# A transformer kernel: smaller first transfers, one scaled half of the values behind a copy, and one group of transposes inside a sum

## The chip, the cores and the metric

The kernel runs on one core of one Trainium2 chip. A core has five engines that run in parallel and meet only at semaphores: TensorE (PE in the profile; its weight loads are PEld), VectorE (DVE), ScalarE (ACT), GpSimd (POOL) and SyncE (SP, which here only issues DMAs). The metric is the device time of one execution in microseconds (us), as the median of several runs.

## The reference, cut to what matters

One call computes a 256 x 1024 activation in fp32 through a feed-forward layer, a mixer of chunked attention and pooling, a second feed-forward layer, and then two more mixers with layer norms: "Fox" attention and "DSA" attention.

```python
x = x + 0.5 * swiglu_ffn(rmsnorm(x, ffn1_norm), w_gate, w_up, w_down)     # starts the kernel
x = x + hybrid_mixer(rmsnorm(x, mix_norm), ...)
x = x + 0.5 * swiglu_ffn(rmsnorm(x, ffn2_norm), ...)
x = rmsnorm(x, final_norm)
# Fox: 8 heads of 128
q, k, v, f_logit, gate = split(x @ fox_w_in)
s = q @ k.T * scale + cum_q - cum_k            # causal
o = softmax(s) @ v
x = layer_norm(DN_ALPHA * x + (silu(gate) * o) @ fox_w_out)
# DSA: top-k selected attention
x = layer_norm(DN_ALPHA * x + dsa_mixer(x))
```

The three places of the change are the very first products (x @ w_gate and x @ w_up), the values v of Fox, and the sum with `fox_w_out` with the transposes of the normalised rows that follow it.

## The kernel before, in words

**Products.** Every fp32 product is made of three: an operand is split into a high part (ACT copies it to a reduced fp32 type: `hi`, `whi`) and the rest (DVE or POOL subtracts: `lo`, `wlo`). A helper `three` makes high x high, high x rest, rest x high. Weights come in chunks of 1 MB, 128 partitions x 2048 columns, into a ring of four buffers `raw`; SP issues a chunk when the rest of the chunk four before it has been made (`lo_ready`), ACT makes `hi` when the chunk has landed and PE has used the chunk four before, DVE makes `lo` behind it, and PE takes the chunk. All engines execute their own program in order: an instruction that waits holds up everything behind it on its engine.

**The start.** The first two chunks (c = 0 and 1) are worked together in pieces along k, the 8 blocks of 128 rows of the contraction: `PIECES = [(0, 1), (1, 1), (2, 2), (4, 2), (6, 2)]`, each a first k and a count. `STEPS` goes over the pieces, and in each over the two chunks. The input arrives already turned, `x_turned`, in four transfers of two k each (256 KB). ACT scales k into `xth` (L1108), DVE makes `xtl` (L1527), ACT makes the piece's `whi` for c = 0 and then for c = 1 (L1213), DVE the two `wlo` (L1651), and PE multiplies in `first_pair` (L585 high, L601 rest). The first weight piece, both chunks together (256 KB), is issued on ACT's queue behind the small constants `sm`; everything else on SP's. While it waits PE executes 9 products of zeros (L660). After the first pair come chunk 2 in two halves, chunk 3, and then the loop. Inside chunk 3 PE turns the row norms into a row (`rstd_to_row`, L505), ACT copies it out of bank 7 (`row`, L1113), and PE waits for that copy (`row_ready`, L572) before it sums into the same bank. On ACT the copy stands behind `hi` of the fifth chunk (L1080).

**Fox attention.** For head h PE makes the scores (`scores2`, L825), DVE adds the bias, negates and takes the row's extreme (`causal`, L1629), ACT makes the exponentials (`exps`, L1183), PE turns them (`turn_probs`, L654), DVE copies them to SBUF (`probs_out`, L1637), and PE multiplies with v (`values2`, L709 to L711). The order on PE is scores of h + 1, turn of h, values of h - 1. v is scaled by the row norms when it leaves PSUM: the first 128 tokens by ACT, the other 128 by DVE (`values_out`, L1798), each in two halves of 512 columns: heads 0 to 3 and heads 4 to 7.

**The end of Fox.** `end_sums` (L517) adds the last half of the contraction for the output matrix in four groups (token tile t, column half nb) of 4 k. Behind it follow the layer norm on DVE (L1884, L1888), transposes of the normalised rows on PE (`turn_y`, L880, four per half), `xth` by ACT (L1343) and `xtl` by DVE (L1844), and then the first DSA product (`one_tile`), which waits for the first half of the parts before k = 0 and for the second before k = 4.

Of the kernel before, what the change touches and what calls it, by code (L numbers as in the profile page):

```python
# [28 lines left out]
KD = D // P  # L29
# [84 lines left out]
def build(nc, a, out):  # L114
    ctx = ExitStack()
    with ctx:
# [133 lines left out]
        sm_landed, xt_landed = sem("sm_landed"), [sem(f"xt_landed{i}") for i in range(KD // 2)]  # L250
# [55 lines left out]
        def _(sp):  # L306
# [15 lines left out]
            def x_piece(k):  # L322
                sp.dma_start(x_turned[:, k:k + 2, :], a["xt"][:, k:k + 2, :]).then_inc(xt_landed[k // 2], 16)
# [6 lines left out]
            weight_piece(1)  # L330
            for i in range(2, len(PIECES) - 1):
                x_piece(PIECES[i][0])
                weight_piece(i)
            x_piece(PIECES[-1][0])
# [67 lines left out]
        def _(pe):  # L402
# [114 lines left out]
            def end_sums(c0, between=None):  # L517

                for t in range(NT):
                    for nb in range(2):  # L520
                        wh, wl = take(c0 + nb)
                        for k in range(HALF):
                            if between and t == 1 and nb == 1 and k == 2:
                                between()
                            m = three(ps[:, 2 * nb + t, :],
                                      xth[:, HALF + k, t * P:(t + 1) * P], xtl[:, HALF + k, t * P:(t + 1) * P],
                                      wh[:, k * BANK:(k + 1) * BANK], wl[:, k * BANK:(k + 1) * BANK], False, k == HALF - 1)
                        m.then_inc(chunk_used if t else acc_part, 1)
# [130 lines left out]
            for _ in range(9):  # L659
                pe.matmul(ps[:, DOWN + 3, 0:P], idle, idle, start=True, stop=True)  # L660
# [187 lines left out]
            def values2(h):  # L848
                if h == 0:
                    pe.wait_ge(v_act, 2)  # L850
                    pe.wait_ge(v_dve, 2)
# [31 lines left out]
            end_sums(C_FO + 2, lambda: turn_y(0, 0))  # L883
            turn_y(0, 1)
# [186 lines left out]
        def _(act):  # L1071
# [145 lines left out]
            cols = first_cols(0)  # L1217
# [4 lines left out]
            for step, (c, i) in enumerate(STEPS):  # L1222
                k, n = PIECES[i]
                if c == 0:
                    act.wait_ge(xt_landed[k // 2], 16)
                    input_hi(0, k, n)
                part_high(c, slice(k * S, (k + n) * S), step if step < N_PARTS else None,
                          part_landed[i] if step < N_PARTS else raw_landed[c], raw_first[:, first_cols(i, c)])
# [278 lines left out]
        def _(dve):  # L1507
# [149 lines left out]
            for step, (c, i) in enumerate(STEPS):  # L1657
                k, n = PIECES[i]
                if c == 0:
                    dve.wait_ge(xt_landed[k // 2], 16)  # L1660
# [151 lines left out]
            values_out(1)  # L1812
# [12 lines left out]
            for h in range(H2):  # L1825
                if h >= 2:
                    causal(h)
                if h >= 1:
                    probs_out(1, h - 1, 2 + (h - 1) % 2)
                if h == 7:  # L1830
# [375 lines left out]
```

## Time and profile before

| | us |
|---|---|
| median of 3 runs | 711.37 |
| lowest and highest of the 3 | 709.96, 712.58 |
| the profiled execution's own time | 709.67 |
| its span on the core | 707.9 |

| engine | busy us | share of the span |
|---|---|---|
| PE | 697.5 | 99% |
| DVE | 480.0 | 68% |
| ACT | 378.3 | 53% |
| POOL | 54.4 | 8% |

The busy time of PE counts overlapping products, so 99% does not say that no stall is left; stalls are found where the start of one product stands further from the start of the one before than its columns explain, or in the idle time that the profile prints in brackets. The granted clock of TensorE is full in all 40 slices of the page. The rows of the places that the change touches stand in a section of their own below.

### The profile page before, as it was taken

The numbers are of one execution on the slowest core, as the hardware profiler recorded it, in microseconds if no ns is written. First come the engines' busy times: TensorE is split into PE (matmuls) and PEld (weight loads), VectorE is DVE, ScalarE is ACT, GpSimd is POOL, SyncE is SP. The second block draws the span as 40 slices with busy tenths as digits, with TensorE's granted clock in tenths as the row PEclk, the third lists the DMA queues.
The fourth block names the chain that finished last, engine by engine and source line by source line (L and its number), as shares of the span: only waits on it lengthen the run. The fifth ranks groups of instructions, "written<-read, shape, count | busy, mean of one in ns | idle before, by whom it ended". The sixth has DMA issues, their size and how long they took to land.

```text
span 707.9 us, 9725 instructions
## 1 busy us (share of the span) xinstructions
PE 697.5 (99%) x3728; PEld 594.3 (84%) x3728; DVE 480.0 (68%) x724; ACT 378.3 (53%) x517; POOL 54.4 (8%) x32
## 2 busy tenths in 40 slices
PE   8999999999999999999999999999999999999995
PEld 7888888888888788888888888888888888888884
DVE  6797777755476556777667755566763738888756
ACT  6865445444377655744455544477444534675450
POOL 0000000000000400000000000000005172130001
PEclk9999999999999999999999999999999999999999
DMA  8987555555355324655455555535573183444001
GB/s 326 357 339 280 203 182 178 186 201 207 119 187 229 120 78 139 258 209 179 178 186 197 205 208 219 177 134 223 186 259 145 42 315 123 176 145 153 1 1 59
DMA packets 21107, 129.33 MB, mean 183 GB/s; under 512 B 2504, under 2 KB 3664, under 8 KB 6864
## 3 DMA queue, kind: packets, MB, share of 16 engines
q1 hardware_dynamic: 19728, 127.51, 49.9%
q10 hardware_dynamic: 1344, 1.34, 0.6%
q8 instruction: 23, 0.38, 0.2%
q14 instruction: 12, 0.10, 0.0%
HBM read 127.79 MB, written 1.06 MB: 182 GB/s over the span
## 4 chain that ended last, share of the span: by engine, by line
PE 98%; DVE 1%; DMA 1%; ACT 0%; issue 0%; ACTq 0%
PE ps L440 24%; PE ps L405 16%; PE ps L407 16%; PE ps L406 16%; PE ps L446 13%; PE ps L425 1%; PE ps L654 1%; PE ps L585 1%; PE ps L1006 1%; PE ps L825 1%; PE ps L459 1%; PE ps L429 1%; DMA raw<-in_first 1%; PE ps L709 1%; PE ps L601 1%; PE ps L710 1%
## 5 line engine op out<-in xcount | busy, mean ns | idle before, releaser
L1514 DVE TENSOR_TENSOR wlo<-raw,whi 128x2048 fp32r<-128x2048 f32 x69 | 159.1, 2313 | 40.7 <-ACT whi L1080 40.5
L440 PE MATMUL ps<-xt,whi 128*128 128x512 f32 x752 | 180.1, 391 | 0.0
L1080 ACT ACTIVATE whi<-raw 128x2048 fp32r<-128x2048 f32 x78 | 148.6, 1908 | 44.9 <-PE ps L407 42.1
L440 PEld LDWEIGHTS ps<-xt,whi 128*128 128x128 f32 x752 | 138.1, 188 | 26.7
L405 PE MATMUL ps<-whi,xt 128*128 128x512 f32 (+1 forms) x304 | 121.6, 400 | 0.1
L407 PE MATMUL ps<-whi,xt 128*128 128x512 f32 (+1 forms) x304 | 116.9, 385 | 0.0
L406 PE MATMUL ps<-wlo,xt 128*128 128x512 f32 (+1 forms) x304 | 116.7, 384 | 0.0
L446 PEld LDWEIGHTS ps<-xt,wlo 128*128 128x128 f32 x752 | 96.4, 191 | 3.7
L446 PE MATMUL ps<-xt,wlo 128*128 128x256 f32 x752 | 97.5, 283 | 0.0
L1467 POOL TENSOR_TENSOR wlo<-raw,whi 128x2048 fp32r<-128x2048 f32 (+1 forms) x9 | 41.1, 4561 | 550.6 <-ACT whi L1080 550.6
L1124 ACT ACTIVATE work<-ps 128x512 f32<-128x512 f32 x44 | 26.2, 597 | 95.1 <-PE ps L440 94.8
L405 PE MATMUL ps<-whi,hth 128*128 128x512 f32 x192 | 75.2, 391 | 0.0
L406 PE MATMUL ps<-wlo,hth 128*128 128x512 f32 x192 | 74.7, 389 | 0.0
L407 PE MATMUL ps<-whi,htl 128*128 128x512 f32 x192 | 74.7, 389 | 0.0
L1597 DVE TENSOR_TENSOR wlo<-raw,whi 128x2048 fp32r<-128x2048 f32 x32 | 73.3, 2292 | 1.5
L405 PEld LDWEIGHTS ps<-whi,xt 128*128 128x128 f32 x304 | 57.2, 188 | 12.4 <-issue 1.7
L407 PEld LDWEIGHTS ps<-whi,xt 128*128 128x128 f32 x304 | 57.1, 188 | 11.7
L406 PEld LDWEIGHTS ps<-wlo,xt 128*128 128x128 f32 x304 | 57.3, 188 | 10.3 <-issue 0.2
L1555 DVE TENSOR_TENSOR work<-ps,work 128x512 f32<-128x512 f32 x44 | 30.2, 689 | 45.5 <-ACT work L1124 45.4
L1159 ACT ACTIVATE whi<-raw 128x2048 fp32r<-128x2048 f32 x32 | 61.1, 1909 | 0.0
L407 PEld LDWEIGHTS ps<-whi,htl 128*128 128x128 f32 x192 | 36.0, 188 | 7.5
L405 PEld LDWEIGHTS ps<-whi,hth 128*128 128x128 f32 x192 | 36.1, 188 | 7.4
(235 smaller groups left out, 692.9 us busy)
## 6 DMA issues: line engine op xcount, KB each, us to landing
raw<-in_gu SPq DMA_DIRECT2D x41, 1024.0 KB, 4.8
raw<-in_dn SPq DMA_DIRECT2D x22, 1024.0 KB, 4.8
raw<-in_win SPq DMA_DIRECT2D x8, 1024.0 KB, 4.8
raw<-in_fqk SPq DMA_DIRECT2D x8, 1024.0 KB, 4.8
raw<-in_wout SPq DMA_DIRECT2D x4, 1024.0 KB, 5.0
raw<-in_fg SPq DMA_DIRECT2D x4, 1024.0 KB, 4.8
raw<-in_fv SPq DMA_DIRECT2D x4, 1024.0 KB, 4.8
raw<-in_fo SPq DMA_DIRECT2D x4, 1024.0 KB, 4.9
```

The lines of the kernel that those rows point to most:

```text
L405: pe.matmul(o, xh, wh, start=start, stop=False)
L406: pe.matmul(o, xh, wl, start=False, stop=False)
L407: return pe.matmul(o, xl, wh, start=False, stop=stop)
L440: return pe.matmul(ps[:, banks[u], :], wh[:, k * S + u * P:k * S + (u + 1) * P], x, start=k == 0, stop=k == KD - 1)
L446: pe.matmul(ps[:, banks[u], S:2 * S], wl[:, k * S + u * P:k * S + (u + 1) * P], xth[:, k, :], start=False, stop=False)
L1080: act.activation(whi[:, c % RING, 0:n], raw[:, c % RING, 0:n], ACT.Copy).then_inc(hi_ready, 1)
L1124: act.activation(gu_sb[:, i % 2, :, :], ps[:, 2 * i:2 * i + 2, S:2 * S], ACT.Copy).then_inc(cross_copied, 1)
L1159: act.activation(whi[:, c % RING, :], raw[:, c % RING, :], ACT.Copy).then_inc(hi_ready, 1)
L1467: pool.tensor_tensor(wlo[:, c % RING, 0:n], raw[:, c % RING, 0:n], whi[:, c % RING, 0:n].bitcast(F32), ALU.subtract).then_inc(lo_ready, 1)
L1514: dve.tensor_tensor(wlo[:, c % RING, 0:n], raw[:, c % RING, 0:n], whi[:, c % RING, 0:n].bitcast(F32), ALU.subtract).then_inc(lo_ready, 1)
L1555: dve.tensor_tensor(g, ps[:, 2 * i:2 * i + 2, 0:S], g, ALU.add).then_inc(gu_read, 1)
L1597: dve.tensor_tensor(wlo[:, c % RING, :], raw[:, c % RING, :], whi[:, c % RING, :].bitcast(F32), ALU.subtract).then_inc(lo_ready, 1)
```

## The change

1. **First step.** The input's transfers follow `PIECES`, so k = 0 and k = 1 come as 128 KB each instead of 256 KB together. The first weight piece is split by chunk: c = 0 (128 KB) stays on ACT's queue, c = 1 (128 KB) goes to SP's with a semaphore of its own, `second_landed`. PE executes 10 products of zeros instead of 9.
2. **Fox values.** DVE's scaling of the second half of v (`values_out(1)`) moves from before the first copy of turned probabilities to behind it, and PE's wait for the second half moves from head 0 to head 4, the first that reads it.
3. **Transposes.** In the last group of `end_sums` the second half's transposes `turn_y(0, 1)` come before k = 3 instead of behind the group; those of the first half stay before k = 2.

```diff
-        sm_landed, xt_landed = sem("sm_landed"), [sem(f"xt_landed{i}") for i in range(KD // 2)]
+        sm_landed, xt_landed = sem("sm_landed"), [sem(f"xt_landed{i}") for i in range(len(PIECES))]
+        second_landed = sem("second_landed")
...
-            def x_piece(k):
-                sp.dma_start(x_turned[:, k:k + 2, :], a["xt"][:, k:k + 2, :]).then_inc(xt_landed[k // 2], 16)
+            def x_piece(i):
+                k, n = PIECES[i]
+                sp.dma_start(x_turned[:, k:k + n, :], a["xt"][:, k:k + n, :]).then_inc(xt_landed[i], 16)
...
             x_piece(0)
-            weight_piece(1)
-            for i in range(2, len(PIECES) - 1):
-                x_piece(PIECES[i][0])
+            cols = first_cols(0, 1)
+            sp.dma_start(raw_first[:, cols], a["first"][:, cols]).then_inc(second_landed, 16)
+            for i in range(1, len(PIECES) - 1):
+                x_piece(i)
                 weight_piece(i)
-            x_piece(PIECES[-1][0])
+            x_piece(len(PIECES) - 1)
...
-                            if between and t == 1 and nb == 1 and k == 2:
-                                between()
+                            if between and t == 1 and nb == 1 and k >= 2:
+                                between(k - 2)
...
-            for _ in range(9):
+            for _ in range(10):
...
-                if h == 0:
+                if h == H2 // 2:
                     pe.wait_ge(v_act, 2)
                     pe.wait_ge(v_dve, 2)
...
-            end_sums(C_FO + 2, lambda: turn_y(0, 0))
-            turn_y(0, 1)
+            end_sums(C_FO + 2, lambda half: turn_y(0, half))
...
-            cols = first_cols(0)
+            cols = first_cols(0, 0)
             act.dma_start(raw_first[:, cols], a["first"][:, cols]).then_inc(part_landed[0], 16)
...
             causal(0)
             causal(1)
-            values_out(1)
...
                     probs_out(1, h - 1, 2 + (h - 1) % 2)
+                if h == 1:
+                    values_out(1)
```

The transfers that SP issues first, before the change (128x512 is 256 KB; `work<-in_xt` is the input, `raw<-in_first` the weight pieces):

```order
1 L323 DMA work<-in_xt 128x512
2 L327 DMA raw<-in_first 128x512
3 L323 DMA work<-in_xt 128x512
4 L327 DMA raw<-in_first 128x1024
5 L323 DMA work<-in_xt 128x512
6 L327 DMA raw<-in_first 128x1024
```

and after it:

```order
1 L325 DMA work<-in_xt 128x256
2 L333 DMA raw<-in_first 128x256
3 L325 DMA work<-in_xt 128x256
4 L329 DMA raw<-in_first 128x512
5 L325 DMA work<-in_xt 128x512
6 L329 DMA raw<-in_first 128x1024
```

SP issues two transfers more ahead of the two-k pieces, and four transfers of the start are now 128 KB: these three and ACT's.

DVE at the end of `causal(1)`, before the change (the ISA rows are `causal`, COPY is `probs_out(0)`, TENSOR_SCALAR is `values_out(1)`):

```order
293 L1629 ISA work,st<-ps,gains 128x256
294 L1629 ISA st 128x1
295 L1798 TENSOR_SCALAR work<-ps,st 128x512
296 L1637 COPY work<-ps 128x384
297 L1629 ISA work,st<-ps,gains 128x128
```

and after it:

```order
293 L1631 ISA work,st<-ps,gains 128x256
294 L1631 ISA st 128x1
295 L1639 COPY work<-ps 128x384
296 L1800 TENSOR_SCALAR work<-ps,st 128x512
297 L1631 ISA work,st<-ps,gains 128x128
```

The copy and the scaling have changed places; both still stand ahead of `causal(2)`.

PE in the last group of `end_sums`, before the change (X is turned by the rows of 128x128 x4; 128x232 is the first DSA product):

```order
1332 L880 MATMUL ps<-eye,X 128x128 x4
1333 L405 MATMUL ps<-whi,xt 128x512
1334 L406 MATMUL ps<-wlo,xt 128x512
1335 L407 MATMUL ps<-whi,xt 128x512
1336 L405 MATMUL ps<-whi,xt 128x512
1337 L406 MATMUL ps<-wlo,xt 128x512
1338 L407 MATMUL ps<-whi,xt 128x512
1339 L880 MATMUL ps<-eye,X 128x128 x4
1340 L405 MATMUL ps<-whi,xt 128x232
```

and after it:

```order
1332 L883 MATMUL ps<-eye,X 128x128 x4
1333 L408 MATMUL ps<-whi,xt 128x512
1334 L409 MATMUL ps<-wlo,xt 128x512
1335 L410 MATMUL ps<-whi,xt 128x512
1336 L883 MATMUL ps<-eye,X 128x128 x4
1337 L408 MATMUL ps<-whi,xt 128x512
1338 L409 MATMUL ps<-wlo,xt 128x512
1339 L410 MATMUL ps<-whi,xt 128x512
1340 L408 MATMUL ps<-whi,xt 128x232
```

The second four transposes stand three products earlier.

## Rows read from the trace of the kernel before

**Rows 1.** The page: busy time per engine, and the chain that ended last.

```profile
PE 697.5 (99%) x3728; PEld 594.3 (84%) x3728; DVE 480.0 (68%) x724; ACT 378.3 (53%) x517; POOL 54.4 (8%) x32
...
PE 98%; DVE 1%; DMA 1%; ACT 0%; issue 0%; ACTq 0%
```

**Rows 2.** Timeline of the start: start us, duration us, engine, line, tiles, [idle before <-releaser].

```profile
5.08 0.51 ACT L1108 ACTIVATE xt<-work,sm 128x256 fp32r<-128x256 f32 x1 [1.91 <-DMA sm<-in_sm]
...
6.21 0.72 ACT L1213 ACTIVATE whi<-raw 128x256 fp32r<-128x256 f32 x2 [0.62 <-DMA raw<-in_first]
...
6.77 0.70 PE L585 MATMUL ps<-xt,whi 128*128 128x512 f32 x2 [1.76 <-ACT whi L1213]
...
9.66 1.08 PE L585 MATMUL ps<-xt,whi 128*128 128x512 f32 x4
```

**Rows 3.** The same timeline: transfers that SP issues.

```profile
2.13 0.43 SPq L327 DMA_DIRECT2D raw<-in_first  x1
...
6.93 0.94 SPq L343 DMA_DIRECT2D X<-in_x  x2
7.91 0.45 SPq L344 DMA_DIRECT2D eye<-in_eye  x1
...
14.55 0.96 SPq L319 DMA_DIRECT2D raw<-in_gu  x2
```

**Rows 4.** DMAs by stretch of issue: count, KB each, us to landing; last, instruction fetches 20.3 to 21.5.

```profile
raw<-in_first SPq DMA_DIRECT2D x1, 512.0 KB, 6.3
...
X<-in_x SPq DMA_DIRECT2D x1, 512.0 KB, 13.2
...
eye<-in_eye SPq DMA_DIRECT2D x1, 128.0 KB, 13.1
...
raw<-in_gu SPq DMA_DIRECT2D x1, 1024.0 KB, 9.7
...
q8 instruction: 1, 0.02, 5.6%
```

**Rows 5.** Timeline of chunk 3: ACT's copy of the row, PE's load behind it.

```profile
24.27 1.91 ACT L1080 ACTIVATE whi<-raw 128x2048 fp32r<-128x2048 f32 x1 [0.93 <-DMA raw<-in_gu]
...
25.44 1.64 PE L425 MATMUL ps<-xt,whi 128*128 128x512 f32 x6
26.09 0.37 ACT L1113 ACTIVATE work<-ps 128x256 f32<-128x256 f32 x1
...
26.51 0.19 PEld L425 LDWEIGHTS ps<-xt,whi 128*128 128x128 f32 x1
```

**Rows 6.** Timeline of Fox heads 0 to 2.

```profile
551.72 0.49 PE L654 MATMUL ps<-eye,work 128*128 128x128 f32 x3
551.92 0.75 DVE L1798 TENSOR_SCALAR work<-ps,st 128x512 f32<-128x512 f32 x1 [4.85 <-PE ps L407]
552.59 0.55 DVE L1637 COPY work<-ps 128x384 f32<-128x384 f32 x1
553.05 0.28 DVE L1629 CUSTOM_DVE_ANT_0 work<-ps,gains 128x128 f32<-128x128 f32 x1
553.25 0.30 PEld L709 LDWEIGHTS ps<-work 128*128 128x128 f32 x2 [0.29 <-issue]
...
554.17 0.19 ACT L1183 ACTIVATION_READ_ACCUMULATOR work<-work,st 128x1 f32 x1
...
554.68 0.49 PE L654 MATMUL ps<-eye,work 128*128 128x128 f32 x3
```

**Rows 7.** Timeline of the end of Fox and the first DSA product.

```profile
586.63 0.75 DVE L1888 SCALAR_TENSOR_TENSOR X<-X,st,gains 128x512 f32<-128x512 f32 x1
...
588.35 0.60 PE L880 MATMUL ps<-eye,X 128*128 128x128 f32 x4
...
589.62 0.69 DVE L1844 TENSOR_TENSOR xt<-ps,xt 128x512 fp32r<-128x512 f32 x1 [0.48 <-ACT xt L1343]
...
590.36 0.19 PEld L405 LDWEIGHTS ps<-whi,xt 128*128 128x128 f32 x1 [0.27 <-DVE xt L1844]
```

More of the change, by code:

```diff
@@ L1224, in _ @@
                 if c == 0:
-                    act.wait_ge(xt_landed[k // 2], 16)
+                    act.wait_ge(xt_landed[i], 16)
                     input_hi(0, k, n)
                 part_high(c, slice(k * S, (k + n) * S), step if step < N_PARTS else None,
-                          part_landed[i] if step < N_PARTS else raw_landed[c], raw_first[:, first_cols(i, c)])
+                          second_landed if step == 1 else part_landed[i] if step < N_PARTS else raw_landed[c], raw_first[:, first_cols(i, c)])
             part_high(2, slice(0, D), N_PARTS, part_landed[len(PIECES) - 1], raw[:, 2, 0:D])
@@ L1659, in _ @@
                 if c == 0:
-                    dve.wait_ge(xt_landed[k // 2], 16)
+                    dve.wait_ge(xt_landed[i], 16)
                     input_lo(0, k, n)
```

## The prediction, made before the changed kernel was run

> **What bounds the kernel now.** I read four views in this order. The page comes first, for who holds the end: the chain that ended last is PE for 98% of the span, and PE's busy time is 99% of it [rows 1]. So only what moves PE's stream counts, and there is little idle time left to win. Then the timeline at the three places of the change, to find PE's stalls there: 1.76 us before the first product [rows 2], 0.29 us before the first product with v [rows 6], and 0.27 us in the first DSA product [rows 7]. Then the DMA view, for when transfers land. Last, the timeline from each place onwards, for the next wait that PE meets: a gain that arrives at a wait which is not itself moved is taken back there. That last look changes the result at the start.
>
> **First step, its own gain.** ACT scales k = 0 at 5.08, released by `sm`, a 24 KB transfer that the change leaves where it is; the first weights land at 6.2 (ACT resumes at 6.21 after 0.62 of idle), and PE starts at 6.77 [rows 2]. With 128 KB of weights on each queue instead of 256, I place their landing at about 5.4 to 5.6: half the bytes, at the rate that I work out below, are 0.33 us less for each of the two pieces that share the engines, and the input's half piece ahead of them another 0.33 at most. The input's path (5.08 plus the 1.69 from there to PE, less the 0.6 us for which ACT sat idle between) then allows PE at about 6.2. The fall is 0.5 to 0.6 us.
>
> PE is not free to run from there. The two-k weight piece was issued at 2.13 and landed 6.3 later, at 8.4 [rows 3, 4]; the same bytes stand ahead of it after the change. PE began on it at 9.66 [rows 2]. Its high part for c = 0 needs about 0.65 us of ACT after 8.4, so PE can begin no earlier than about 9.2: **at most 0.46 us** is left at this point.
>
> **First step, what takes it back.** In chunk 3 PE waits for ACT's copy of the norm row, since it sums into the same bank. That copy stands on ACT behind `hi` of the fifth chunk, which ran from 24.27, when the chunk had landed (0.93 of idle before it, released by the DMA), for 1.91 us; the copy ran from 26.09 to 26.46, and PE's next weight load starts at 26.51 [rows 5]. The group of six products ends at 27.08 and one lasts 0.39, so the sixth starts at 26.69, no later than its pitch asks: the wait costs nothing now but sits exactly at PE's heels. After the change PE arrives 0.46 earlier, ACT does not: the fifth chunk is issued at 14.55 and lands 9.7 later, at 24.25 [rows 3, 4], at the end of a queue that has been full since the start. When PE has waited, the product goes almost with its load, so the sixth can go at 26.54: about **0.14 us** of the 0.46 survives.
>
> The landing itself moves too, the wrong way. Four 128 KB transfers with 1 KB rows replace two 256 KB ones with 2 KB rows. The nearest row is `eye`, 128 KB in 1 KB rows: issued at 7.91, landed at 21.0, where the second half of X, issued at 7.42, landed at 20.6 [rows 3, 4]. That is 0.4 us, with 0.1 of rounding. Between the landings at 8.4 and 20.6 lie 4.5 MB, 2.7 us for 1 MB or 0.33 us for 128 KB. So a 1 KB-row piece costs 0 to 0.17 us more, four of them 0 to 0.7 us at the bounds; I take 0.15 in all, from the lower part, since the first two land while the engines aren't yet filled. First step together: -0.14 + 0.15, **about 0**.
>
> The Trainium skill's page "DMA: Bandwidth & Descriptors", section "Why small descriptors are slow (HBM only)", speaks against this part of the change: each packet carries about 3 cycles beside one per 32 bytes. By that, an estimate: 35 cycles instead of 32 for 1 KB, 67 instead of 64 for 2 KB, 4.5% of the 1.3 us of those 512 KB, 0.06 us; the sum below would then be 0.09 lower. No row of before shows it finer than the 0.1 of `eye`.
>
> The tenth product of zeros ends about 0.2 us later than the ninth; PE idles 1.76 us there [rows 2], so it is hidden, and would not be if data came before 5.3.
>
> **Fox values.** Now: DVE is released at 551.92, scales the second half of v until 552.67, copies the turned probabilities of head 0 from 552.59 to 553.14, starts `causal(2)` at 553.05, and PE loads for the values of head 0 at 553.25 after 0.29 idle [rows 6]. After: the copy waits for PE's transposes, which end at 552.21 [rows 6], runs 552.25 to 552.80, and PE, free to load at 552.96 (553.25 less the idle 0.29), doesn't wait: about 0.25 us gained. But `causal(2)` still stands behind both operations, and these no longer start at 551.92 but at 552.25. It starts at 552.25 + 0.47 + 0.67 = 553.39, 0.34 later than now. Behind it hang ACT's exponentials of head 2, done 1.31 us after `causal(2)` began (553.05 to 554.36), and PE's transposes of head 2, now 0.32 after that, at 554.68, with no wait [rows 6]. A load follows by 0.11 what it waited for (553.25 behind the copy's end at 553.14), and the product by some hundredths, so the transposes go at 553.39 + 1.31 + 0.15 = 554.85. The stall of 0.25 is gone, one of 0.48 stands a head later, net +0.17. In the heads behind, DVE has more to do per head than PE (copy, `causal`, a reciprocal and two gates) and sets the pace, and part of its own delay is made up while it waits for PE's scores before `causal(3)`. Carrying the starts of both engines through heads 3 to 6 leaves, by my estimate, half of the 0.17: **+0.09 us**. Bounds: -0.25, if the delay of `causal(2)` is hidden, and +0.17.
>
> **Transposes.** Now the second four transposes stand at 588.35, DVE makes the rest at 589.62 after 0.48 idle, and PE's load for k = 4 starts at 590.36 after 0.27 idle, released by it [rows 7]. Three products of 0.23 earlier, they go at about 587.65. The normalised half is ready at 586.63 + 0.75 = 587.38 [rows 7], and PE's load comes at 587.43: they pass with 0.05 to spare. The rest then is ready near 589.8, and PE reaches k = 4 at 590.12. The first half isn't touched, and PE's own work is the same, so the stall goes and nothing takes its place: **-0.24 us**, bounds -0.27 and 0. Nothing waits behind the group's end in these 0.44 us: the residual of its columns is later on DVE.
>
> **The sum.** 0 + 0.09 - 0.24 = -0.15 us. The profiled execution took 709.67, its span 707.9; it would become 709.5. The median of the three runs is 711.37, 1.7 above the profiled execution, and I apply the difference to it: **711.2 us**. The three runs lie 2.6 us apart, far more than the effect.
>
> **Rivals.**
>
> *The fifth chunk lands in time.* An instruction fetch of 16 KB kept one DMA engine busy at 20.4 for about 1 us (5.6% of 16 engines over 1.2 us) [rows 4], which is a reason why that landing is late. If the fetch falls elsewhere, the copy of the row comes earlier and the full 0.46 survives: -0.46 + 0.09 - 0.24 = -0.6, 710.8 us. Against it: the fetch follows the program, and that is nearly the same. Chance 0.2.
>
> *Slower: 1 KB rows cost as much as 2 KB rows.* Then 512 KB of the start take the time of 1 MB, 1.3 us more, the fifth chunk lands 1.3 later, and PE stalls for it at the row copy: -0.14 + 1.3 + 0.09 - 0.24 = +1.0, 712.4 us. It turns the result from a delay of the landing of 0.3 us. `eye` speaks against the full price, not against a third of it. Chance 0.15.
>
> *Fox gains.* ACT's exponentials hide the later `causal(2)`: 0 - 0.25 - 0.24 = -0.5, 710.9 us. Against it: the exponentials follow within 0.3 us of it. Chance 0.1.
>
> *The transposes don't do what they are moved for.* The second normalised half comes more than 0.05 late and PE waits in the middle of the group, which ends the sum later and delays the first half too: the 0.24 is not gained, +0.1, 711.5 us. Chance 0.1.
>
> *The forecast.* 711.2 us, chance 0.45.
>
> **The numbers.** All cases lie between 710.8 and 712.4. The scatter of a median is added: the three runs stand 1.4 below and 1.2 above theirs. I give 709.4 to 712.9. A measurement of this kernel can tell about 0.5%, 3.6 us, from no change; no case reaches it, so faster 0.03, same 0.95, slower 0.02 for what I haven't seen.
>
> **What the next profile would show.** Right: first product near 6.2; the two-k piece begun near 9.2; the weight load behind ACT's copy of the row now with idle time of some 0.3 before it, and PE's place there within 0.2 us of today's; no idle before the values of head 0, but one of 0.4 to 0.5 before the transposes of head 2; no idle before k = 4 of the first DSA product. Wrong: the loop's first product more than 0.3 us earlier or later than today, the transposes of head 2 without a wait, or a wait of PE inside the last group of `end_sums`. A difference of medians above 2 us would say that something else moved.

## The result, and the profile after

| | before | after |
|---|---|---|
| median, us (10 runs each, same chip) | 711.28 | 712.62 |
| lowest and highest | 709.62, 712.58 | 710.46, 713.04 |
| profiled execution | 709.67 | 713.01 |
| its span | 707.9 | 711.2 |

The ratio after to before is 1.0025, 95% interval 1.0015 to 1.0034. The change made the kernel 1.3 us slower. The time lies inside the range, but the forecast was 0.15 us faster, and the measurement excludes that: it tells 0.1% apart, where the prediction had allowed for 0.5%.

**The page.** PE still holds the end, as in [rows 1]. In the chain that ended last, by line, the first weights have a share of 1%, as they have before: a loss of this size doesn't show on the page, and the places of the change have to be read one by one.

```profile
PE 699.3 (98%) x3730; PEld 596.0 (84%) x3730; DVE 480.2 (68%) x724; ACT 378.7 (53%) x517; POOL 54.4 (8%) x32
...
PE ps L443 24%; PE ps L408 16%; PE ps L410 16%; PE ps L409 16%; PE ps L449 13%; PE ps L428 1%; PE ps L657 1%; DMA raw<-in_first 1%; PE ps L588 1%; PE ps L1008 1%; PE ps L462 1%; PE ps L432 1%; PE ps L828 1%; PE ps L517 0%; PE ps L712 0%; PE ps L713 0%
```

**The start.** The timeline of the changed kernel, answering to [rows 2] (columns as there; L588 is the high product, L1110 ACT's scaling of the input, L1215 its high part of the weights):

```profile
3.41 0.51 ACT L1110 ACTIVATE xt<-work,sm 128x256 fp32r<-128x256 f32 x1 [0.23 <-DMA sm<-in_sm]
...
4.34 0.72 ACT L1215 ACTIVATE whi<-raw 128x256 fp32r<-128x256 f32 x2 [0.43 <-DMA raw<-in_first]
4.50 2.15 SPq L325 DMA_DIRECT2D work<-in_xt  x1
...
5.34 0.71 PE L588 MATMUL ps<-xt,whi 128*128 128x512 f32 x2
...
9.49 0.91 ACT L1110 ACTIVATE xt<-work,sm 128x256 fp32r<-128x256 f32 x2 [3.39 <-DMA work<-in_xt]
...
10.80 1.15 ACT L1215 ACTIVATE whi<-raw 128x512 fp32r<-128x512 f32 x2 [0.40 <-DMA raw<-in_first]
...
11.58 1.55 PE L588 MATMUL ps<-xt,whi 128*128 128x512 f32 x4 [3.20 <-ACT whi L1215]
```

The first product goes 1.43 us earlier than before (5.34, 6.77). The piece behind it goes 1.92 later (11.58, 9.66): PE has used up k = 0 and k = 1 and sits idle for 3.20 us, because both the input and the weights for k = 2, 3 are late. ACT waits 3.39 us for the input, scales it, and waits 0.40 more for the weights, until 10.80; that wait ends last. The input is the transfer that SP issued at 1.66 before, and issues at 2.60 now. The DMA view, for transfers issued at those two moments (KB, us from issue to landing), before and then after, and last the weights, issued at 3.08 after:

```profile
work<-in_xt SPq DMA_DIRECT2D x1, 256.0 KB, 5.3
```

```profile
work<-in_xt SPq DMA_DIRECT2D x1, 256.0 KB, 6.9
```

```profile
raw<-in_first SPq DMA_DIRECT2D x1, 512.0 KB, 7.7
```

The input landed at 7.0 before and lands at 9.5 now; the weights landed at 8.4 [rows 3, 4] and land at 10.8. The busy time by stretch (us, then PE, PEld, DVE, ACT, POOL, the granted clock, the DMA engines' share, GB/s) tells more, before and then after:

```profile
4.50:7.00 2.50, 0.74 (x5) 0.58 (x5) 0.82 (x2) 1.29 (x4) 0.00 (x0) 1.00 1.02 342
8.00:12.00 4.00, 4.00 (x24) 3.45 (x23) 3.71 (x9) 3.59 (x8) 0.00 (x0) 1.00 1.04 405
12.00:16.00 4.00, 4.00 (x26) 3.55 (x25) 3.57 (x7) 3.50 (x7) 0.00 (x0) 1.00 1.04 423
```

```profile
4.50:7.00 2.50, 2.50 (x15) 2.32 (x15) 1.96 (x6) 1.60 (x5) 0.00 (x0) 1.00 0.71 128
8.00:12.00 4.00, 0.80 (x5) 0.59 (x4) 1.42 (x3) 2.10 (x5) 0.00 (x0) 1.00 1.00 389
12.00:16.00 4.00, 4.00 (x16) 3.38 (x15) 4.00 (x9) 3.73 (x8) 0.00 (x0) 0.57 1.05 420
```

Two things stand there. Between 4.5 and 7 us the DMA engines move 128 GB/s instead of 342, with plenty of work issued; SP's issue at 4.50 takes 2.15 us, where a single one took at most 0.73 before. I call this **the stall**. And between 12 and 16 the granted clock is 0.57, after PE's idle 3.20 us: mostly the lower of its two levels (1.2 GHz), with 16 products where 26 went before. PE, 1.92 us late at its first product after the idle time, is 3.55 late when the clock is back (16.00, where the same products went at 12.45), and stays so until Fox.

**Why the two profiles lie 3.3 us apart and the medians 1.3.** The times of before form groups: of the 31 runs beside the first set of experiments, 10 lie at 709.7 to 710.1, 18 at 711.2 to 712.0, three above. The profile of before is one of the first group and has no stretch at half clock after its first product; an execution of 711.54 (of the kernel with the Fox edit alone, below) has one. The median of before contains this cost already. In the changed kernel nine of ten times lie at 712.2 to 713.0, as that of the profile with the half clock; that they all have it is read from the times, since one was profiled. The tenth, 710.46, lies under every run of the start alone below, and what was different in it is not shown.

**Fox.** The timeline around heads 0 and 2, answering to [rows 6] (L1800 scales v, L1631 is `causal`, L712 the values, L657 the transposes):

```profile
556.28 0.74 DVE L1800 TENSOR_SCALAR work<-ps,st 128x512 f32<-128x512 f32 x1
556.48 0.30 PEld L712 LDWEIGHTS ps<-work 128*128 128x128 f32 x2
...
556.94 0.28 DVE L1631 CUSTOM_DVE_ANT_0 work<-ps,gains 128x128 f32<-128x128 f32 x1
...
558.36 0.31 PEld L657 LDWEIGHTS ps<-eye,work 128*128 128x128 f32 x3 [0.68 <-DVE work L1639]
558.39 0.52 PE L657 MATMUL ps<-eye,work 128*128 128x128 f32 x3 [0.31 <-ACT work L1185]
```

The load for the values of head 0 has no idle time in front any more, and the transposes of head 2 now wait for ACT's exponentials. Laid on each other, the two streams of PE stand 3.56 us apart before Fox, 3.24 at the values, 3.74 at these transposes, and 3.67 by head 4: +0.11 us. (These are the starts of the same products in the two profiles: 555.28 and 551.72, 556.81 and 553.57, 558.97 and 555.23.)

**Transposes.** The end of the last group, answering to [rows 7] (L1891 normalises, L883 turns, L1847 makes the second half's rest):

```profile
590.31 0.75 DVE L1891 SCALAR_TENSOR_TENSOR X<-X,st,gains 128x512 f32<-128x512 f32 x1
...
591.33 0.49 PE L883 MATMUL ps<-eye,X 128*128 128x128 f32 x3
591.52 0.69 DVE L1847 TENSOR_TENSOR xt<-ps,xt 128x512 fp32r<-128x512 f32 x1 [0.46 <-ACT xt L1345]
...
592.72 0.68 DVE L1847 TENSOR_TENSOR xt<-ps,xt 128x512 fp32r<-128x512 f32 x1
...
593.70 0.19 PEld L408 LDWEIGHTS ps<-whi,xt 128*128 128x128 f32 x1
```

The load for k = 4, which waited 0.27, stands at 593.70 with no idle time, 0.3 after the rest that it needs. The distance of the streams falls from 3.67 to 3.34: -0.33 us.

### The profile page after: what moved, and what is told of

It reads as the page before. It is cut to its first block, busy times and chain, and to the rows that moved or that the text cites. A ratio compares the mean times of both kernels' runs of the same rounds, so it can differ in the third digit from the quotient of the medians.

```text
span 711.2 us, 9731 instructions
## 1 busy us (share of the span) xinstructions
PE 699.3 (98%) x3730; PEld 596.0 (84%) x3730; DVE 480.2 (68%) x724; ACT 378.7 (53%) x517; POOL 54.4 (8%) x32
## 4 chain that ended last, share of the span: by engine, by line
PE 97%; DMA 1%; DVE 1%; SPq 0%; ACT 0%; issue 0%
PE ps L443 24%; PE ps L408 16%; PE ps L410 16%; PE ps L409 16%; PE ps L449 13%; PE ps L428 1%; PE ps L657 1%; DMA raw<-in_first 1%; PE ps L588 1%; PE ps L1008 1%; PE ps L462 1%; PE ps L432 1%; PE ps L828 1%; PE ps L517 0%; PE ps L712 0%; PE ps L713 0%
## 5 line engine op out<-in xcount | busy, mean ns | idle before, releaser
L409 PEld LDWEIGHTS ps<-wlo,hth 128*128 128x128 f32 x192 | 36.0, 188 | 7.4
```

The lines of the kernel that those rows point to most:

```text
L409: pe.matmul(o, xh, wl, start=False, stop=False)
```

## The experiments

All are compared with the kernel before on the same chip in the same set; its median lay between 711.28 and 711.40 in every set, so kernels of different sets can be compared too. "Part 1" is the first step's edit. For each kernel the landings of the input and of the weights for k = 2, 3 come from one profile. One of the twelve executions of Fox only took 1811 us and is not in its ratio. The comparisons with before:

| run | edit | median, us | ratio, 95% interval | input lands | weights land |
|---|---|---|---|---|---|
| start only | part 1 | 712.93 | 1.0032 (1.0019 to 1.0045) | 9.4 | 10.7 |
| Fox only | part 2 | 711.55 | 1.0004 (0.9992 to 1.0015) | | |
| transposes only | part 3 | 711.06 | 0.9995 (0.9983 to 1.0007) | | |
| bridge | part 1, PE kept busy | 712.04 | 1.0011 (1.0002 to 1.0021) | 8.9 | 10.8 |
| input split | half of part 1 | 709.73 | 0.9981 (0.9971 to 0.9991) | 7.2 | 8.6 |
| weights split | the other half | 710.06 | 0.9987 (0.9977 to 0.9996) | 7.2 | 8.5 |
| input singles | part 1, all input in 128 KB | 712.30 | 1.0008 (0.9998 to 1.0018) | 9.5 | 10.8 |
| 16 zeros | part 3, 16 products of zeros | 709.64 | 0.9978 (0.9968 to 0.9988) | | |
| held back | part 1, SP waits | 712.59 | 1.0018 (1.0009 to 1.0027) | 8.7 | 10.1 |
| pair on ACT | part 1, other queue | 709.89 | 0.9984 (0.9975 to 0.9994) | 7.6 | 8.9 |
| ACT filled | part 1, k = 1 weights on ACT | 710.68 | 1.0002 (0.9992 to 1.0012) | 8.1 | 9.4 |
| delay | part 1, all transfers later | 714.13 | 1.0055 (1.0036 to 1.0074) | 10.7 | 12.0 |
| order | part 1, SP's order | 710.61 | 0.9998 (0.9987 to 1.0008) | 8.0 | 9.4 |
| all, pair on ACT | whole change, other queue | 709.54 | 0.9983 (0.9974 to 0.9992) | 7.3 | 8.8 |
| best | input split, part 3, 12 zeros | 709.38 | 0.9979 (0.9971 to 0.9988) | 7.1 | 9.0 |

### Which part costs the time

One part each, against the kernel before. The start alone is part 1 of the diff above, with its tenth product of zeros.

> The first step's new transfers and the tenth product of zeros alone, on the kernel before. Theory A (the loss is at the start: the two-k pieces land late, PE starves before k = 2 for about 3 us and its clock then stands at half for 3.4 us, which together set the start back by 3.5 us in the changed kernel's profile): slower than before by 1.4 to 1.8 us in the median, nearly all of the change's loss and a little more, since the other two parts together gain 0.2; the profile shows PE idle for 2 us or more before its fifth step. Theory B (the loss comes from Fox and from code that moved elsewhere, and the profiled start is an accident of one execution): within 0.4 us of before.

> The moved scaling of the second half of v and PE's moved wait alone. Theory A: +0.1 us, as the shift of PE's stream through the heads shows in the two profiles (0.32 gained before the values of head 0, 0.50 lost before the transposes of head 2, 0.07 made up in the heads behind). Theory B: +0.5 us or more.

> The second half's transposes before k = 3 of the last group alone. Theory A: -0.3 us (the two profiles show PE's stream 0.33 us earlier behind this place); no idle before k = 4 of the first DSA product. Rival: 0, if the wait comes back at the next layer-norm half.

The start alone gives 712.93, as much as the whole change; its eight runs scatter more, and the three slowest (713.67 to 714.82) were not profiled. Fox alone and the transposes alone cannot be told from before; what their traces show (+0.11, -0.33) lies below what these runs resolve. The start alone, its stretches and the product behind the idle time:

```profile
4.50:7.00 2.50, 2.50 (x11) 2.31 (x11) 2.07 (x6) 1.77 (x5) 0.00 (x0) 1.00 0.52 140
...
12.00:16.00 4.00, 4.00 (x25) 3.51 (x24) 3.76 (x9) 3.62 (x8) 0.00 (x0) 1.00 1.05 422
```

```profile
11.45 1.17 PE L588 MATMUL ps<-xt,whi 128*128 128x512 f32 x4 [2.28 <-ACT whi L1216]
```

The stall is there with part 1 alone, and this execution (711.57, the shortest of its eight) had the full clock behind PE's idle time. (Its first two products still took 1.20 us where the changed kernel's took 0.71; the wait for the landing swallows that.) So the late landing alone takes 711.57 - 709.67 = 1.9 us against before's profile, and the rest up to the changed kernel's 713.01 comes with the half clock. The Fox kernel's profile of 711.54 shows the half clock of the group near 711.4, without a late landing:

```profile
8.00:12.00 4.00, 4.00 (x15) 3.34 (x15) 3.64 (x10) 3.60 (x9) 0.00 (x0) 0.61 1.04 404
```

### The clock's share

Part 1, and PE multiplies zeros between the second and the third piece, so that the late landing leaves no idle time.

```diff
+                        if step == 4:
+                            for _ in range(12):
+                                pe.matmul(ps[:, DOWN + 3, 0:P], idle, idle, start=True, stop=True)
```

> Part one alone, with 12 more products of zeros (about 2.6 us at full clock) on PE between its fourth and its fifth step, where it starved. They keep PE busy and compute nothing. If the half clock behind the starvation is what costs, the clock stays full there and the kernel gains 1.4 to 1.7 us against part one alone in executions that starve, so it comes within 0.5 us of before. If the late pieces alone cost (the clock's share is small), it stays 1.4 or more above before. If the starvation is rare, the zeros delay PE and it is slower than part one alone by up to 2.6.

```profile
8.76 2.84 PE L592 MATMUL ps<-XN 128*128 128x128 f32 x24
```

```profile
12.00:16.00 4.00, 4.00 (x25) 3.52 (x24) 3.67 (x9) 3.66 (x8) 0.00 (x0) 1.00 1.05 417
```

The clock stays full and the median falls from 712.93 to 712.04. 0.9 us of the start's cost hang on the half clock, less than the 1.4 to 1.7 that I had expected, and the stall's own price stays: no run of this kernel is under 711.2, where before has a third of its runs under 710.2. Like is to be compared with like: by the groups of their times, runs at full clock go from about 709.9 to about 711.7 (1.8 us; 2.1 to the bridge's median, in which PE goes on at 11.59 instead of 11.45), runs with the stretch from about 711.4 to about 712.7 (1.3 us).

The kernel before has idle time of its own in front of its first product, 1.76 us [rows 2]. This run fills it, with part 3 and

```diff
-            for _ in range(9):
+            for _ in range(16):
```

> The start as before with 16 products of zeros instead of 9, which end near 6.4 where the first product starts at 6.8, and the moved transposes. If half of the executions of before lose 1.6 us to a stretch of half clock that the idle time before the first product brings, as the two groups of its times (709.7 to 710.1 and 711.2 to 711.7) say, the slower group goes and the median falls by about 1.6 to 709.6. If the clock has nothing to do with that idle time: the median falls by 0.3 alone.

```profile
1.06 5.56 PE L660 MATMUL ps<-XN 128*128 128x128 f32 x32 [1.06 <-DVE st L1654]
6.88 0.70 PE L585 MATMUL ps<-xt,whi 128*128 128x512 f32 x2 [0.26 <-ACT whi L1212]
```

The first product goes 0.1 us later and the median falls by 1.7 against before, by 1.4 against the transposes alone: all nine runs lie between 709.50 and 710.11, the groups near 711.4 and 712.5 are gone. With nine products of zeros and the same part 3 the runs lay between 709.37 and 712.38. So those groups come from what PE does in front of its first product. Seven more products of zeros do two things, fill the idle time and keep PE at work longer, and the profiles show that both can matter. In the Fox kernel's the clock falls again after the idle time. The profile of the transposes alone (712.38, of the slowest group) is another case: the products of zeros end at 5.27, and the real products from 7.08 on go at half pace, until about 13 us. Its products between 8 and 12 us, a pair of them, and the same pair in the kernel before:

```profile
8.00:12.00 4.00, 4.00 (x14) 3.35 (x13) 3.62 (x9) 3.11 (x7) 0.00 (x0) 1.00 1.00 366
```

```profile
8.50 1.05 PE L585 MATMUL ps<-xt,whi 128*128 128x512 f32 x2
```

```profile
8.26 0.62 PE L585 MATMUL ps<-xt,whi 128*128 128x512 f32 x2
```

14 products where 24 went before, a pair in 1.05 us where it took 0.62, and PE is 3.0 us late when it is fast (15.43, 12.45). The granted clock reads 1.00 all the same, so at the start of a trace that column alone does not show that PE is fast; the products have to be timed.

### Which half of part 1 brings the stall

The input in 128 KB pieces for k = 0 and 1, the first weights unsplit on ACT's queue (no `second_landed`); then the reverse, the weights split over the two queues and the input in two-k pieces as before.

> Half of part one: the input's k = 0 and k = 1 as 128 KB each, the first weights unsplit on ACT's queue as before. Theory C (the transfers of the input with 2 KB rows are slow whenever they run early, and the smaller ones only move that slow stretch behind the first products): the input of k = 0 lands near 3.3, the two-k input of k = 2 and 3 at 8.5 or later (6.96 before), PE starves before k = 2, and the kernel is 1 us or more slower than before. Theory D (too many transfers queued at once, the weights' split included, jam the queue): the two-k input lands by 8, and the time is within 0.7 us of before.

> The other half of part one: the first weights split by chunk over the two queues, the input in two-k transfers as before. Theory C: the first input transfer stays slow (landing near 4.9 with sm at 5.1), nothing starves behind it, within 0.4 us of before. Theory D: the queue holds one transfer more and the two-k input behind it lands late, 0.7 us or more slower.

**Each half alone makes the kernel faster**, 709.73 and 710.06. Theory C fails in the first, where nothing lands late, and both fail in the second, which neither had faster. In both the input for k = 2, 3, issued at 2.13, lands 5.1 later:

```profile
work<-in_xt SPq DMA_DIRECT2D x1, 256.0 KB, 5.1
```

The input split, PE's two waits at the start:

```profile
5.62 0.70 PE L585 MATMUL ps<-xt,whi 128*128 128x512 f32 x2 [0.85 <-ACT whi L1213]
...
9.36 1.17 PE L585 MATMUL ps<-xt,whi 128*128 128x512 f32 x4 [0.71 <-ACT whi L1213]
```

The first product is 1.15 us earlier than before, the second pair 0.3. As predicted, most of an earlier first product is lost at the next landing. The median still falls by 1.6. With 0.85 us of idle time instead of 1.76 six of nine runs lie below 709.8, so by their times most escape the half clock; only one was profiled.

### What the stall is not

*Rows of 2 KB.* Part 1, with every two-k input piece as two transfers of 128 KB, each on the same semaphore (waits for `16 * n`).

```diff
-                sp.dma_start(x_turned[:, k:k + n, :], a["xt"][:, k:k + n, :]).then_inc(xt_landed[i], 16)
+                for j in range(k, k + n):
+                    sp.dma_start(x_turned[:, j:j + 1, :], a["xt"][:, j:j + 1, :]).then_inc(xt_landed[i], 16)
```

> All of part one, and every input transfer of two k issued as two of one k (1 KB rows), so that no input transfer has 2 KB rows; three more issues on SP. Theory C: the slow stretch behind 5.3 us goes, the input of k = 2 and 3 lands before 7.5, PE's idle before its fifth step falls under 1 us, and the kernel is within 0.5 us of before or faster. Theory D: more transfers are queued, so the input lands at 9 or later and the kernel is 1.5 us or more slower than before.

The single for k = 3, 128 KB in 1 KB rows, issued at 3.08:

```profile
work<-in_xt SPq DMA_DIRECT2D x1, 128.0 KB, 6.4
```

Such a piece took 2.5 us at the head of the queue and is caught here like any other; the engines move 176 GB/s between 4.5 and 7 us. The size of the input's rows isn't it.

*SP too far ahead.* Part 1, and SP waits for the last small weight piece before it issues the input for k = 2, 3:

```diff
             for i in range(1, len(PIECES) - 1):
+                if i == 2:
+                    sp.wait_ge(second_landed, 16)
                 x_piece(i)
```

> Part 1 alone, as in the run of the start alone, and SP waits until the second 128 KB weight piece has landed (4.1 us there) before it issues the two-k input piece k=2,3 and all behind it. Theory jam (the four small transfers let SP run ahead, the queues fill up, and the engines stall): with nothing queued behind the first five transfers the stall goes; no SP issue takes over 1 us, x(2,3), issued at 4.1 to 4.3, lands by 7.5, the 512 KB piece by 9.3, time 709.7 to 710.5. Rival (between 5 and 6.5 us the engines move little whenever the small transfers have run out early, however many are queued): x(2,3) lands at 9 or later again, time 712 to 713.

```profile
4.20 0.33 SPq L325 DMA_DIRECT2D work<-in_xt  x1
```

```profile
4.50:7.00 2.50, 2.50 (x15) 2.32 (x15) 1.98 (x6) 1.65 (x5) 0.00 (x0) 1.00 0.59 109
```

My theory of a jam of queued transfers falls. The 109 GB/s of the window are in part want of work, for what was still under way at 4.20 landed by 5.4, and the landing at 8.7 owes something to the later issue. But in the slices of 0.3 us from 6.0 to 6.9 the engines move 61 to 75 GB/s, with 256 KB issued at 4.20, 512 KB at 4.57 and more behind. The time is 712.59. The runs of this kernel part cleanly: four at 711.4 to 711.9 with a mean granted clock of 0.997 or 0.998 over the execution, six at 712.6 to 713.0 with 0.995 or 0.996.

*The time since launch.* Part 1, and SP and ACT issue nothing before PE's third product of zeros:

```diff
+                if n == 2:
+                    m.then_inc(delayed, 1)
...
+            sp.wait_ge(delayed, 1)
             x_piece(0)
...
+            act.wait_ge(delayed, 1)
             act.dma_start(sm[:, :], a["sm"]).then_inc(sm_landed, 16)
```

> Part 1 alone, and SP and ACT issue their first transfer only when PE has done its third zero product, about 1.5 us later (2.3 us instead of 0.75). If the stall goes by the time since launch: the engines' slow stretch stays at 4.8 to 7 us, now amid the small transfers, and the first pieces land late instead of x(2,3). If it goes by the transfers: every landing and the slow stretch shift by 1.5 us together (x0 4.8, slow from 6.3, x(2,3) near 11), and the time is 1 to 1.5 us over the 712.93 of the start alone.

```profile
4.60 0.43 SPq L326 DMA_DIRECT2D work<-in_xt  x1
```

```profile
work<-in_xt SPq DMA_DIRECT2D x1, 256.0 KB, 6.1
```

The transfers begin at 2.74, 2.0 us later; the first input piece lands at 5.2 instead of 3.2, and the one for k = 2, 3 at 10.7 instead of 9.4. The rate in slices of 0.3 us from 0 to 12:

```profile
GB/s 0 0 0 0 0 0 0 0 0 0 0 0 48 208 135 233 352 342 376 260 273 266 212 178 137 143 116 137 150 171 253 218 294 355 396 382 389 369 369 294
```

The slow stretch runs from 6.9 to 9.0 (116 to 178 GB/s), where the changed kernel has it from 4.8 to 6.9 (68 to 150): it moved by as much as the transfers, 2.1 us, and is less deep, which is why the landing moved by 1.3 only. It is tied to the transfers and not to a moment of the launch. The time, 714.13, is the median of four runs.

### What the stall goes by

Part 1, with the second 128 KB weight piece on ACT's queue behind the first:

```diff
-            cols = first_cols(0, 1)
-            sp.dma_start(raw_first[:, cols], a["first"][:, cols]).then_inc(second_landed, 16)
...
-            cols = first_cols(0, 0)
-            act.dma_start(raw_first[:, cols], a["first"][:, cols]).then_inc(part_landed[0], 16)
+            for c, landed in enumerate((part_landed[0], second_landed)):
+                cols = first_cols(0, c)
+                act.dma_start(raw_first[:, cols], a["first"][:, cols]).then_inc(landed, 16)
```

> Part 1 with the second 128 KB weight piece on ACT's queue behind the first instead of on SP's. The number and size of the transfers is that of the changed kernel, SP has one less. If it is the number of small transfers at the head that brings the stall: x(2,3) lands at 9 us or later and the time is 712 to 713. If it is what SP's queue holds: SP's queue is as in the kernel with the input alone split (709.7), x(2,3) lands by 7.5, time 709.6 to 710.3.

```profile
4.50:7.00 2.50, 2.21 (x11) 1.66 (x10) 0.96 (x3) 1.52 (x4) 0.00 (x0) 1.00 0.85 281
```

The same transfers, of the same sizes, one of them on another queue: 281 GB/s instead of 140 in that stretch, and 709.89 instead of 712.93, all ten runs within 0.15 us. So the number of small transfers isn't the cause either. The edit changes two things, though: the piece's queue, and with it the order on SP's, where the input for k = 1 now follows that for k = 0 directly. Two further runs ask what about the queues matters. In the first the 256 KB weights of k = 1 go to ACT's queue, and the second small piece stays on SP's:

```diff
                 x_piece(i)
-                weight_piece(i)
+                if i > 1:
+                    weight_piece(i)
...
+            cols = first_cols(1)
+            act.dma_start(raw_first[:, cols], a["first"][:, cols]).then_inc(part_landed[1], 16)
```

> Part 1 alone with the 256 KB weight piece of k=1 on ACT's queue behind its 128 KB piece; SP has x0, the second 128 KB weight piece, x1, x(2,3), and so on. Theory two queues (the engines stall when ACT's queue has run dry, at 4.3 us in the changed kernel and only at 5.0 to 6.4 in the ones without a stall): ACT's queue now lasts to about 5.5, x(2,3) lands by 7.8, time 709.5 to 710.5. Rival (it goes by the second weight piece behind x0 on SP's queue, that is by both kinds of 128 KB transfer on one queue): x(2,3) lands at 9 or later, time 711.5 to 713.

```profile
4.50:7.00 2.50, 2.50 (x11) 2.31 (x11) 2.11 (x6) 1.74 (x5) 0.00 (x0) 1.00 0.81 220
```

In the second only the order on SP's queue changes: the input for k = 1 before the second weight piece.

```diff
-            cols = first_cols(0, 1)
-            sp.dma_start(raw_first[:, cols], a["first"][:, cols]).then_inc(second_landed, 16)
             for i in range(1, len(PIECES) - 1):
                 x_piece(i)
+                if i == 1:
+                    cols = first_cols(0, 1)
+                    sp.dma_start(raw_first[:, cols], a["first"][:, cols]).then_inc(second_landed, 16)
                 weight_piece(i)
```

> Part 1 alone with SP's second and third transfer exchanged: x0, x1, then the second 128 KB weight piece. Sizes, number and queues are those of the changed kernel. Theory two queues: ACT's queue runs dry at 4.3 us as before, the stall stays, x(2,3) lands at 9 or later, 712 to 713. Rival (order on SP's queue: what matters is that two pieces of the input stand at its head, as in the runs without the stall at 709.7 and 709.9): x(2,3) lands by 7.8, time 709.7 to 710.5.

```profile
4.50:7.00 2.50, 2.08 (x13) 1.72 (x13) 1.89 (x5) 2.21 (x6) 0.00 (x0) 1.00 0.83 235
```

```profile
10.19 1.17 PE L589 MATMUL ps<-xt,whi 128*128 128x512 f32 x4 [1.49 <-ACT whi L1217]
```

Both give half of the cure (220 and 235 GB/s, landing at 8.1 and 8.0, medians 710.68 and 710.61), and neither the one nor the other theory had said half. Filling ACT's queue longer helps, and so does another order on SP's with ACT's untouched: a queue that runs dry is not the whole cause, nor is the order.

### The versions that beat both kernels

The whole changed kernel with that one transfer on ACT's queue and 12 products of zeros instead of 10; and the kernel before with the input split, part 3, and 12 products of zeros instead of 9.

> The whole changed kernel, with the second 128 KB weight piece on ACT's queue instead of SP's, and 12 zero products instead of 10. If the start is all that made the change slower, the other two parts keep their +0.11 and -0.33 us of the trace: median 709.5 to 709.8, ratio to before 0.9975 to 0.998. If the parts work on each other in another way it stays above 710.5.

> The kernel before with three edits: the input's first two-k piece in two 128 KB transfers (709.73 alone), 12 zero products instead of 9 (they end at about 5.5 us, where the first product started at 5.62), and the transposes moved as in the change (0.3 us in the trace). The effects add in part: the late group of times near 711.4 is gone, median 709.2 to 709.6, ratio to before 0.997. If the split's and the zero products' gain are the same gain, the clock's, it is 709.5 as with the zero products alone; if the split shifts the start by its 1.1 us, 709.0.

709.54 and 709.38: 1.7 to 2 us under the kernel before, 3.1 and 3.2 under the changed one. The first of them is the strongest evidence for where the changed kernel lost its time: it differs from the change in that transfer's queue and in two products of zeros, and the pair on ACT, with ten, shows that the transfer alone does most of it (709.89 against 712.93). The second hit its expectation, in which the effects add only in part.

## Why the prediction was wrong

**What bounds the kernel: right**, and so was the place to look; the two waits at the start decided the result. **Of the first step** the early gain was even larger than I said: first product at 5.34, not 6.2, since the small pieces landed at 3.2 and 4.3 where I had placed the weights at 5.4 to 5.6, and the constants `sm`, which I had left at their place, at 3.4 instead of 5.1. So the tenth product of zeros was not hidden: the first product started at 5.34 with no idle time before it, 1.00 after ACT began its high part of the weights, where it took 0.56 before. It cost nothing in the end. I had worked from the rate of full engines (0.33 us for 128 KB); a small transfer at the head of the queue landed 2.5 to 3.1 us after its issue where the 256 KB piece took 5.0 on ACT's queue.

**The step that failed** is the next: "landed 6.3 later, at 8.4; the same bytes stand ahead of it after the change", from which I let PE begin its next piece at about 9.2 and put the gain there at 0.46 at most. The landing was taken over from before as if it hung on bytes alone. The piece landed at 10.8, its input at 9.5 instead of 7.0, and PE began it at 11.58: 1.92 us lost in place of 0.46 gained. That the order and the queues of the transfers ahead could slow them all stood in no term, and the bound to the other side was made from `eye` alone, that is from the transfer's own rows. The rival on the slow side had the right sign with another mechanism: 1 KB rows are not dear, for the input singles, with six more such pieces, took 712.30 where the start alone took 712.93. Its 712.4 lies near the 712.62 by accident. So does the range hold it in part by luck: its upper end, 712.9, isn't even what its rule gives (712.4 + 1.2 = 713.6).

The Trainium skill's page "DMA: Bandwidth & Descriptors", section "Rules for kernel authors", says that spreading transfers over the issuing engines doesn't help the bandwidth and saves only issue time, since they share the 16 engines. The pair of runs above (140 against 281 GB/s for one small transfer moved between queues) speaks against it for these first microseconds, though with the order on SP's queue changed alone the engines already move 235. Once the engines are full it holds here: every kernel whose stretch I read, the delayed one (373) excepted, moves 417 to 431 GB/s between 12 and 16 us.

**The row copy in chunk 3** took nothing back, for PE came 3.5 us late to it and not 0.46 early. Whether it would have is not shown.

**The clock** stood in no term either. At full clock throughout the start costs 1.8 to 2.1 us; the stretch at half clock costs either kernel another 1 to 1.6, and by the groups of the times before pays it, or more, in two of three runs, the changed kernel in nine of ten. Applying the difference of 1.7 between the profile of before and its median as if it were scatter was a mistake of reading: it was a stretch at half clock that the profiled execution had been spared. Seen so, it was the largest thing to be had at the start (1.4 us of the median, with seven products of zeros).

**Fox: right.** +0.09 predicted, +0.11 in the traces; the stall of head 0 is gone, that before the transposes of head 2 is there (PE 3.24 late before it, 3.74 after), and heads 3 and 4 make up part. I predicted idle time of 0.4 to 0.5 there (the 0.48 of the working should have been 0.42, the 0.25 gained and the 0.17 lost); PE's is 0.31, the load's 0.68.

**Transposes: right**, -0.24 predicted, -0.33 in the traces, beyond the bound of -0.27 by 0.06. The small gap of 0.05 to the normalised half held.

## What to carry to other kernels

Where transfers are made smaller or moved between queues at a kernel's start, the landing of those behind them is a term of its own, to be measured and not taken over; try each half of such an edit alone, for here two halves that each gain 1.3 to 1.6 us lose 1.5 together. Before working on waits of a tenth of a microsecond, look at whether the times form groups, and fill the idle time in front of the first product with products of zeros until data come: seven more of them were worth 1.4 us of the median (711.06 to 709.64). A median and a profiled execution from different groups are not to be joined by a constant. At the start of a trace, time the first products themselves instead of trusting the granted clock's column.

## What the runs showed of the hardware

**The stall.** With the input in 128 KB pieces, and the second small weight piece behind the first of them on SP's queue, the DMA engines move 109 to 176 GB/s between 4.5 and 7 us (changed kernel 128, start alone 140, bridge 146, input singles 176, held back 109), and 220 where ACT's queue also has the weights of k = 1, against 281 to 342 in before, the pair on ACT's queue and the two halves; an issue on SP takes up to 2.15 us. It moves with the transfers (by 2.1 us for 2.0), and is not tied to the time since launch, the size of the input's rows, the number of transfers, or how far SP runs ahead. One observation goes with it in the profiles. The rate in 40 slices of the first 12 us, 0.3 us each, of before, of the changed kernel and of the pair on ACT's queue:

```profile
GB/s 0 0 0 0 0 27 114 133 195 190 85 95 291 333 381 417 410 362 362 348 335 253 287 253 389 416 389 430 396 375 341 416 410 410 396 403 437 417 416 430
```

```profile
GB/s 0 0 0 0 0 10 169 194 207 324 304 372 270 297 290 246 137 89 96 68 116 75 150 178 253 273 287 280 294 376 437 437 382 376 430 396 430 396 423 403
```

```profile
GB/s 0 0 0 0 0 3 100 232 108 141 183 255 266 361 395 355 342 277 246 219 266 225 335 307 259 382 355 410 362 382 369 307 389 382 403 403 403 423 410 423
```

Where the stall is deep, there is no dip near 3 us (the changed kernel has 207 to 372 GB/s from 2.4 to 3.6, the first piece lands at 3.2) and a long one from 4.8. Where it is absent, a short dip comes first (85 and 108 at the least, first piece at 4.9 and 4.6), while PE still multiplies zeros, and the engines are fast from then on. The two are not bound to each other: the run with the other order on SP's queue dips to 97 GB/s at 2.4 us and still has half of the stall. Why is open; no run looked into the memory side.

**The clock.** Nine products of zeros and then idle time of 1.8 us are followed by products at half pace in two of three executions, by their times; sixteen with 0.26 us of idle time in none of nine, and ten with 0.29 us (the pair on ACT's queue) in none of ten. Two ways are seen in profiles: the granted clock falls to half after the idle time (0.61 between 8 and 12 us, 711.54), or PE isn't fast before about 13 us though the column reads 1.00 (712.38). Not every run of the group near 711.4 shows a lower mean clock (0.994 to 0.998 over the execution), so some of them may belong to the second way with an earlier rise; that is not shown.
